# Expert weights in larger transfers: the up part whole, and the later experts in one transfer of 3 MB

## The reference, cut to what matters

```python
def hier_moe(x, w_group, b_group, w_router, b_router, w_e1, w_e3, w_e2):
    ...
    for gi in range(N_GROUPS):
        h = jax.nn.silu(jnp.einsum('md,edf->mef', xt, w_e1[gi])) * jnp.einsum('md,edf->mef', xt, w_e3[gi])
        out = out + jnp.einsum('mef,efd->md', h * combine[:, gi, :, None], w_e2[gi])
    return out.reshape(n, t, d)
...
    x2 = layer_norm(DEEPNORM_ALPHA * x1 + y, g_ln2, b_ln2)
```

## Time and profile before

| | us |
|---|---|
| median of 3 runs | 880.46 (879.99 to 881.18) |
| the profiled execution | 881.31 |
| its span, from the first instruction to the last | 879.50 |

### The profile page before, as it was taken

One profiled execution on the slowest core, in us unless ns is written; L12 is line 12 of the kernel. 1 busy time (PEld: TensorE's weight loads), 2 busy tenths in 40 slices (PEclk: granted clock), 3 DMA queues, 4 the chain that ended last, 5 costly groups with the idle time before them and its releaser, 6 DMA issues.

```text
span 879.5 us, 11914 instructions
## 1 busy us (share of the span) xinstructions
PE 766.8 (87%) x4710; PEld 556.6 (63%) x4710; DVE 360.8 (41%) x630; ACT 226.5 (26%) x439; POOL 158.0 (18%) x159
## 2 busy tenths in 40 slices
PE   6999999999799999999999999991899999276730
PEld 6999985775466999999999974551333343022210
DVE  4899927988676411110110104358221211111128
ACT  5213321735577622222221210010111101000013
POOL 4000001000312334343334310001201111100000
PEclk9999999999899999999999999995799999789885
DMA  8423124112100452222222139744899999999955
GB/s 326 141 79 102 56 84 154 62 54 52 48 2 1 180 204 84 73 85 84 84 89 81 48 107 427 291 167 192 318 417 423 423 425 424 425 426 426 418 208 196
DMA packets 37811, 173.37 MB, mean 197 GB/s; under 512 B 6985, under 2 KB 7545, under 8 KB 25337
## 3 DMA queue, kind: packets, MB, share of 16 engines
q1 hardware_dynamic: 32840, 161.30, 47.8%
q0 software_dynamic: 4912, 11.28, 3.4%
HBM read 162.07 MB, written 16.78 MB: 203 GB/s over the span
## 4 chain that ended last, share of the span: by engine, by line
PE 74%; DMA 8%; SPq 7%; DVE 6%; issue 2%; ACT 1%; POOLq 0%; ACTq 0%
PE PS L685 39%; PE PS L987 7%; PE PS L877 7%; DMA expert<-in_w_e 6%; PE PS L668 5%; SPq L499 4%; PE PS L1008 3%; PE PS L795 2%; SPq L502 2%; PE PS L761 2%; PE PS L775 2%; PE PS L743 2%; PE PS L838 1%; PE PS L941 1%; DVE expert_out L1743 1%
## 5 line engine op out<-in xcount | busy, mean ns | idle before, releaser
L685 PE MATMUL PS<-x_hi,w_hi 128*128 128x288 f32 (+2 forms) x656 | 142.5, 299 | 9.3 <-DVE x_lo L1325 8.5
L685 PE MATMUL PS<-x_lo,w_hi 128*128 128x288 f32 (+2 forms) x656 | 142.0, 298 | 0.0
L987 PE MATMUL PS<-expert,moe_tmp 128*64 128x512 f32 (+2 forms) x576 | 114.5, 644 | 31.6 <-DMA expert<-in_w_e 30.1
L685 PE MATMUL PS<-x_hi,w_lo 128*128 128x288 f32 (+2 forms) x656 | 141.8, 298 | 0.0
L685 PEld LDWEIGHTS PS<-x_hi,w_hi 128*128 128x128 f32 x656 | 106.9, 192 | 9.7 <-POOL w_lo L459 8.4
L1078 ACT ACTIVATE w_hi<-raw_ring 128x1024 fp32r<-128x1024 f32 (+1 forms) x57 | 57.0, 1001 | 214.5 <-PE PS L685 210.2
L685 PEld LDWEIGHTS PS<-x_lo,w_hi 128*128 128x128 f32 x656 | 106.8, 191 | 0.0
L685 PEld LDWEIGHTS PS<-x_hi,w_lo 128*128 128x128 f32 x656 | 106.7, 191 | 0.0
L987 PEld LDWEIGHTS PS<-expert,moe_tmp 128*64 128x64 f32 (+2 forms) x576 | 36.6, 136 | 99.0 <-issue 96.9
L459 POOL TENSOR_TENSOR w_lo<-raw_ring,w_hi 128x1024 fp32r<-128x1024 f32 (+1 forms) x33 | 70.1, 2124 | 136.5 <-ACT w_hi L1078 136.5
L1342 DVE SCALAR_TENSOR_TENSOR conv_z<-attn_tmp,wdw,conv_z 128x576 f32<-128x576 f32 x120 | 90.6, 811 | 0.3
(11 more groups left out here) (296 smaller groups left out, 1011.0 us busy)
## 6 DMA issues: line engine op xcount, KB each, us to landing
expert<-in_w_e SPq DMA_DIRECT2D x96, 1024.0 KB, 26.6
raw_ring<-in_w_gate_t SPq DMA_DIRECT2D x24, 512.0 KB, 3.3
raw_ring<-in_w_glu_t SPq DMA_DIRECT2D x8, 512.0 KB, 4.4
raw_ring<-in_w_como_t SPq DMA_DIRECT2D x8, 512.0 KB, 3.4
heads<-in_w_out SPq DMA_DIRECT2D x1, 4096.0 KB, 13.9
x_rows<-x_tiles SPq DMA_DIRECT2D x8, 512.0 KB, 5.0
expert_out<-expert_rows SPq DMA_DIRECT2D x8, 512.0 KB, 6.4
x_raw<-in_xT SPq DMA_DIRECT2D x4, 576.0 KB, 6.1
```

The lines of the kernel that those rows point to most:

```text
L685: mm = pe.matmul(half(name, s, 128, cols[s]), w[:, n % 2, at + 128 * k:at + 128 * k + 128], x[:, k, t0[s]:t0[s] + cols[s]], start=(k == 0 ...
L987: mm = pe.matmul(PS[r0:r0 + nr, 2, :].rearrange("p (s f) -> p s f", s=2), xgT[:, k, r0:r0 + nr], w13[s % NB][:, :, k, :], start=(k == 0), ...
```

## The change

The two arrays of expert weights, `w_e13` and `w_e2`, become one array `w_e` with rows of 6144 numbers (24 KB), up part first. Three ways to load follow:

- Experts 19 to 31 (the list `WHOLE`: those that follow in the buffers of units 6 and later) come in one transfer of 3 MB with rows of 24 KB. It is issued behind `e_y` of the unit that used the buffer, where the down part was issued.
- Experts 7 and 8 (`HALVED`: those that follow in the buffers of unit 0) are loaded as before, up part in two halves behind `e_h_first` and `e_h`.
- All others have the up part in one transfer of 2 MB with rows of 16 KB. For experts 9 to 18 it is issued behind `e_h`, where the second half was; the down part is as before.

TensorE waits before k = 0 for the whole of what it has been given: the whole up part, or for `WHOLE` all 3 MB; `result_step` then has no wait for the down part.

```diff
+WHOLE = [s + NB for u in range(6, NS) for s, _, _ in STAGES[u][1] if s + NB < NE]
+HALVED = [s + NB for s, _, _ in STAGES[0][1]]
...
+            def load_expert_up(e, b):
+                return sp.dma_start(we[b][:, 0:4096], a["w_e"][bass.ds(e, 1), :, 0:4096].rearrange("a p n -> p (a n)")).then_inc(we13[b], 16)
...
+            def load_expert(e, b):
+                return sp.dma_start(we[b][:, 0:6144], a["w_e"][bass.ds(e, 1)].rearrange("a p n -> p (a n)")).then_inc(we13[b], 16)
...
             for u in range(NS + 1):
                 if u < NS:
...
                             expert_at[s + NB] = sp.value_load(order[0:1, r:r + 1], min_val=0, max_val=NE - 1)
-                            sp.wait_ge(e_h_first, u + 1)
-                            load_expert_up(expert_at[s + NB], s % NB, 0)
-                    for s, _, _ in STAGES[u][1]:
-                        if s + NB < NE:
-                            sp.wait_ge(e_h, u + 1)
-                            load_expert_up(expert_at[s + NB], s % NB, 1)
+                            if u == 0:
+                                sp.wait_ge(e_h_first, 1)
+                                load_expert_first(expert_at[s + NB], s + NB)
+                            elif s + NB not in WHOLE:
+                                sp.wait_ge(e_h, u + 1)
+                                load_expert_up(expert_at[s + NB], s % NB)
+                    if u == 0:
+                        for s in HALVED:
+                            sp.wait_ge(e_h, 1)
+                            load_expert_second(expert_at[s], s)
                 if u >= 1:
                     for s, _, _ in STAGES[u - 1][1]:
                         if s + NB < NE:
                             sp.wait_ge(e_y, u)
-                            load_expert_down(expert_at[s + NB], s % NB)
+                            if s + NB in WHOLE:
+                                load_expert(expert_at[s + NB], s % NB)
+                            else:
+                                load_expert_down(expert_at[s + NB], s % NB)
...
                 for k in range(KT):
-                    if k % 4 == 0:
-                        for s, _, _ in members(u):
-                            pe.wait_ge(we13[k // 4][s % NB], 16 * (s // NB + 1))
+                    for s, _, _ in members(u):
+                        if k == 0:
+                            pe.wait_ge(we13[s % NB], 16 * (s // NB + 1))
+                        if k == 4 and s in HALVED:
+                            pe.wait_ge(we13_second[s], 16)
...
                 for s, _, _ in members(u):
-                    pe.wait_ge(we2[s % NB], 16 * (s // NB + 1))
+                    if s not in WHOLE:
+                        pe.wait_ge(we2[s % NB], 16 * (s // NB + 1))
```

More of the change, by code:

```diff
@@ L359, in program @@
         flag_ready = sem("flag_ready")
-        we13 = [[sem(f"we13_{n}_{i}") for i in range(NB)] for n in range(2)]
+        we13 = [sem(f"we13_{i}") for i in range(NB)]
+        we13_second = {s: sem(f"we13_second_{s}") for s in HALVED}
         we2 = [sem(f"we2_{i}") for i in range(NB)]
@@ L494, in src, with load_expert_first, load_expert_second @@
                 return a["w_xo_t"][j]
[L497 to L499 removed]
+            def load_expert_up(e, b):
+                return sp.dma_start(we[b][:, 0:4096], a["w_e"][bass.ds(e, 1), :, 0:4096].rearrange("a p n -> p (a n)")).then_inc(we13[b], 16)
+            def load_expert_first(e, s):
+                b = s % NB
+                return sp.dma_start(we[b][:, 0:2048], a["w_e"][bass.ds(e, 1), :, 0:2048].rearrange("a p n -> p (a n)")).then_inc(we13[b], 16)
+            def load_expert_second(e, s):
+                return sp.dma_start(we[s % NB][:, 2048:4096], a["w_e"][bass.ds(e, 1), :, 2048:4096].rearrange("a p n -> p (a n)")).then_inc(we13_second[s], 16)
+            def load_expert(e, b):
+                return sp.dma_start(we[b][:, 0:6144], a["w_e"][bass.ds(e, 1)].rearrange("a p n -> p (a n)")).then_inc(we13[b], 16)
             def load_expert_down(e, b):
[L502 removed]
+                return sp.dma_start(we[b][:, 4096:6144], a["w_e"][bass.ds(e, 1), :, 4096:6144].rearrange("a p n -> p (a n)")).then_inc(we2[b], 16)
             sp.dma_start(ring[:, 0, :], src("glu_b0")).then_inc(ring_full[0], 16)
@@ L553, in _ @@
             for s in range(4):
-                load_expert_up(s, s, 0)
-                load_expert_up(s, s, 1)
+                load_expert_up(s, s)
                 load_expert_down(s, s)
@@ L565, in _ @@
                     wait_job(sp, "c4")
-                    load_expert_up(4, 4, 0)
-                    load_expert_up(4, 4, 1)
+                    load_expert_up(4, 4)
                     load_expert_down(4, 4)
@@ L571, in _ @@
                     sp.dma_start(x1_d[c * T + t0:c * T + t0 + nr], x1[0:nr, tt, :]).then_inc(x1_out, 16)
-            load_expert_up(5, 5, 0)
-            load_expert_up(5, 5, 1)
+            load_expert_up(5, 5)
             load_expert_down(5, 5)
@@ L582, in _ @@
             wait_job(sp, "t4")
-            load_expert_up(e, N_FIXED, 0)
-            load_expert_up(e, N_FIXED, 1)
+            load_expert_up(e, N_FIXED)
             load_expert_down(e, N_FIXED)
@@ L988, in hidden_step @@
                                        w13[s % NB][:, :, k, :], start=(k == 0), stop=(k == KT - 1))
-                    if k == 3:
+                    if u == 0 and k == 3:
                         mm.then_inc(e_h_first, 1)
@@ L1953, in lay_out @@
     up = np.stack([x["w_e1"].reshape(NE, KT, 128, FE), x["w_e3"].reshape(NE, KT, 128, FE)], 1)
-    r["w_e13"] = up.transpose(0, 3, 2, 1, 4).reshape(NE, 128, 2 * KT * FE)
-    r["w_e2"] = x["w_e2"].reshape(NE, 2, 128, D).transpose(0, 2, 1, 3).reshape(NE, 128, 2 * D)
+    up = up.transpose(0, 3, 2, 1, 4).reshape(NE, 128, 2 * KT * FE)
+    r["w_e"] = np.concatenate([up, x["w_e2"].reshape(NE, 2, 128, D).transpose(0, 2, 1, 3).reshape(NE, 128, 2 * D)], 2)
     return r
```

8 lines of the change are left out of this document (2 added, 6 removed).

## The result

| | us | against before |
|---|---|---|
| median of 4 runs, changed kernel | 903.14 (902.09 to 906.49) | 1.028 [1.0256, 1.0305] |
| median of 4 runs, kernel before | 880.23 (877.05 to 881.18) | |
| the profiled execution, changed | 902.32, span 900.50 | 881.31, span 879.50 |

The change costs 22.9 us by the medians; 18.5 were forecast. The forecast of 899.0 is 4.1 us short, and the range reached 906.

What follows compares the result with a forecast made beforehand. From 642 us an unpausing weight stream was taken as the bound, TensorE keeping up. 1.5 + 9.1 + 10.9 - 3.0 = 18.5 us on 881.3 gave 899.8, 899.0 as median; forecast band 895 to 904, range 888.5 to 906.

Steps and rivals of the forecast that it cites:

- pause at unit 11: Experts 26 and 27 wait for unit 10's result, behind unit 11's hidden product; stream pauses 9.1 us.
- end: After the last landing, unit 14's hidden product, unit 13's result and a turn still precede the last result: 10.9 us longer.
- early: Up parts of experts 9 and 10 issued 3.5 us later, near 641 us; mostly covered, 1.5 us taken.
- rate: Rows of 16 and 24 KB make the weight stream faster: 3 us gained, bounds 0 and 4.7.
- Nothing: List of parts costing 0, among them fewer transfers and waits, the array's layout, and gathers, hidden even at threefold time.
- the indirect transfers suffer behind them: Rival: large rows are slower, or gathers and scatters suffer behind them; above 905 us, chance 0.12.
- the instruction queue's packets: Only 16 KB packets in the trace, 1.1 us each; at that rate 61 MB cost 120 us more; given little weight.
- A gain a transfer: Rival: each transfer costs something in the stream, so fewer are faster; no change at 0.58 us each; chance 0.08.
- No pause: Rival: the stream does not pause at unit 11, only end, start and rate count; about 890 us, chance 0.14.

Runs made afterwards that it cites:

- e9: Changed kernel, but GpSimd issues each unit's scatter before waiting for the previous scatter and gathering into its buffer: ratio 1.0232.
- e4: Changed kernel, but up parts of experts 26 and 27 are issued behind 24 and 25 without waiting for unit 10's result: ratio 1.0214.
- e5: Changed kernel, but on TensorE and VectorE the result of unit u - 1 comes before the rows of unit u + 1: ratio 1.0197.
- e3: Changed kernel, but experts 28 to 31 come as four up parts of 2 MB, then four down parts of 1 MB: ratio 1.0195.
- e6: Kernel of e2, but three transfers of 1 MB replace each of 3 MB, same place, TensorE waiting for all three: ratio 1.0283.
- e1: Changed kernel without 3 MB transfers: up parts whole (2 MB) behind the hidden product, down parts behind the result: 878.44 us, ratio 0.9978.
- e2: Changed kernel with the array stored as three blocks, so the same transfers move in rows of 8 KB: ratio 1.0247.

## Why the prediction was right and where it was wrong

The time lies in the range and in the 895 to 904 of the forecast. The pause at unit 11 and the end, which carry the sum, are there as described. That the time is so near is in part luck: a pause of 6.8 us that the prediction had put at nothing was partly offset by terms that came out smaller than forecast, by 2.7 us at unit 11 and 1.0 at the start, and by one of 1.7 us that it did not have (below).

By the terms of its sum, in us (measured from the stretches and the timeline of the changed kernel, and from e9 where a term could be had alone):

| term | forecast | measured | from |
|---|---|---|---|
| early | +1.5 | +0.5 | share 0.92 against 0.94 in the 25 us from the first hidden product on |
| pause at unit 11 | +9.1 | +6.4 (alone +10.0) | stretch 788 to 804; e9 |
| pause at unit 9 and 10 | 0 | +6.8 | stretch 744 to 762 |
| end | +10.9 | +11.0 | 860.33 - 848.04 = 12.3, before 1.3 |
| rate | -3.0 | -1.9 | 102 us at 427 against 423 GB/s, some 85 us at 430 against 426 |
| sum | +18.5 | +22.8 | measured in all: +23.4 |

0.6 us of the 23.4 stay without a term, but the terms are less exact than that. Around a pause the packets that still run are slower (rows of 24 KB take 1.01 and 1.06 us on average in these two stretches, 0.91 in a full one), so by bytes the two pauses are larger: 18 x (1 - 237/430) = 8.1 and 16 x (1 - 220/430) = 7.8 us. And one term is missing: the parameters of the last normalisation. SyncE issues them behind unit 12's result, before the change at 828.0 us, while weights still flow: 1.7 us of each engine's time goes to them ahead of the last weight packet, and the first of their two transfers lands at 837.1, ahead of the weights that were issued at 812.2 and land at 838.9. So transfers of one queue need not land in the order of their issue. Now they are issued at 846.6, and the stream is free of them. With both, the sum is 0.5 + 7.8 + 8.1 + 11.0 - 1.9 - 1.7 = 23.8 us, 0.4 over.

The profiled execution then is 21.0 us longer, since the experts begin 3.3 us earlier and what follows the last result takes 0.9 us more (40.2 against 39.3).

**The step that failed** is in the paragraph "Nothing": the gathers, "whose last is issued at 770.6, 50 us ahead of its unit, and land in 8.7 us, so that even a threefold time stays hidden". Landings of 13 to 18 us, against up to 12.0 before, opened a pause; 18 us is not much over twice the 8.7, far from threefold. The step looked at one gather, the last, and asked how late it could be. It should have looked at the loop that issues them. In the trace of before GpSimd's gathers wait 97.8 us in all, ten times, for a scatter to land; 9.8 us each, with 2.3 us for issuing gather and scatter, is 12.1 us a turn, against TensorE's 12.0 a unit from start to start (the prediction's 12.3 adds up lengths that overlap a little). The gather of unit 10 was issued at 720.64 and needed at 736.16, so 3.5 us were to spare even for a landing of 12.0. That unit 14's gather was 50 us early only shows that the stream held TensorE back from unit 11 on. The rival "the indirect transfers suffer behind them" named the first half of the mechanism, with 0.12 and a time above 905; its own cost was smaller, 4 us net (e9 has 4.0 us less idle time than the changed kernel), because part of the first pause shortens the second.

**The pause at unit 11** was right in place and cause (e4 fills the stretch, e9 shows the pause with the first one gone). Its size was 0.9 us short alone. Why e5 has only 4.9 us of it stays open. In the changed kernel itself it is smaller than forecast, since the stream comes late to unit 11 already.

**The end** was right in each step: one hidden product right behind the last landing (0.14 us), 7.09 + 3.64 + turn and release, 12.2 us forecast and 12.3 measured. e3 takes 7.3 us of it away by the order of the bytes.

**Early**: the issue for experts 9 and 10 is at 637.14, 19.1 us after the first hidden product, against 16.4 before: 2.7 us later, not 3.5, since unit 0's hidden product took 9.28 us here and 9.96 before (granted clock 0.91 and 0.88 in those 25 us). The queue covers most of it.

**The rate** was below my choice, and inside its bounds of 0 and 4.7. In full stretches a row of 4, 8, 16 and 24 KB keeps an engine for 159, 309, some 612 and 912 ns, which is about 9 ns a row and 150 ns for each 4 KB. The prediction took the fixed part from the GB/s of two stretches, 0.13 us for the 128 rows more that 1 MB has with rows of 4 KB, so 16 ns a row on each engine; that was nearly twice too large. Over the whole stream the weights' packets take 194.4 us of each engine in both kernels, since those beside the pauses are slower, so the gain shows only where the stream is full. For the long rows the chosen side was the right one; the instruction queue's packets say nothing of the weights'.

**A gain a transfer** is refuted by e6: three for one, and no loss beyond the error. The rule of the Trainium skill that was weighed for it ("SBUF — State Buffer", section "The DMA setup-cost knee (why "@ 1 MiB" ≠ asymptote)"), to move as much as possible in one transfer, doesn't carry over to this queue with several transfers in flight; no run here shows a gain of its size.

**No pause** was refuted: the stream stopped at unit 11, as the count of buffers said.

## What to carry to other kernels

When a change makes anything in a shared resource slower, look for loops that it closes, and compare the loop's turn with the pace of the consumer: a lead of several buffers covers a single late transfer, not a turn that is longer than the pace. A larger transfer that must wait for the whole of its buffer gives up the early half of the release; here that cost a pause, and the last bytes in the wrong order cost 11 us, of which e3 took back 7, against some 2 us for the longer rows. Merging is harmless where the queue covers the later release, as with the up part's halves, which were released 3.5 us apart (e1, -0.2%). Keep last in the stream what is used last.

## What the runs showed of the hardware

- **Long rows on one queue slow small transfers on another.** Gathers and scatters of 4 KB rows landed in at most 12.0 us beside weights with rows of 8 KB (12.1 in e2, which differs from the changed kernel in the row length alone), 14.9 where the longest rows were of 16 KB (e1) and 20.2 where they were of 24 KB (24.2 in e9, for a gather that goes out 2.4 us after a scatter).
- **Rows beyond 8 KB bring little.** A full stream moves 423 to 427 GB/s with 8 KB rows in the stretches of the kernel before and 430 to 432 with 24 KB, 1 to 2%. The fixed part of a row, some 9 ns of the 309 ns of a row of 8 KB, leaves little more to gain.
- **A transfer costs nothing of its own in a full queue**: 26 more of them in the stream (e6 against e2) left the time that SyncE's packets take on each engine the same (196.7 against 197.5 us).
